# A modulation product moved from TensorE's narrow tiles to VectorE, one half of it

## The reference, cut to what matters

```python
mod = jnp.einsum('bd,de->be', jax.nn.silu(c), w_ada[l]) + b_ada[l]
sh1, sc1, g1, sh2, sc2, g2 = [m[:, None, :] for m in jnp.split(mod, 6, axis=-1)]
h = _rms(x, norm1_g[l]) * (1.0 + sc1) + sh1
```

## Time and profile before

| what | value |
|---|---|
| median of 3 runs | 1909.57 us (1907.05 to 1909.94) |
| profiled execution, its span | 1910.2 us |
| TensorE busy | 1819.2 us (95%) |
| VectorE busy | 601.7 us (31%) |
| ScalarE busy | 477.1 us (25%) |
| read from main memory | 579.96 MB |

### The profile page before, as it was taken

One profiled execution on the slowest core, in us unless ns is written; L12 is line 12 of the kernel. 1 busy time (PEld: TensorE's weight loads), 2 busy tenths in 40 slices (PEclk: granted clock), 3 DMA queues, 4 the chain that ended last, 5 costly groups with the idle time before them and its releaser, 6 DMA issues.

```text
span 1910.2 us, 27104 instructions
## 1 busy us (share of the span) xinstructions
PE 1819.2 (95%) x11233; PEld 1032.4 (54%) x11233; DVE 601.7 (31%) x1224; ACT 477.1 (25%) x800; POOL 351.5 (18%) x306
## 2 busy tenths in 40 slices
PE   8999999999998899999999999999999898899998
PEld 8987999777976333323332233322322697644443
DVE  6777555337566300100010000000000787501112
ACT  5854443325322110000000010000000565322121
POOL 3000000000000599999940000000000100100000
PEclk9998999998999999999999999999999899999999
DMA  6555657446733999999999999999999451579996
GB/s 196 156 142 185 198 197 239 153 134 212 263 111 132 394 419 415 420 419 420 412 418 420 420 418 408 419 420 420 415 418 402 111 168 62 220 308 420 420 419 281
DMA packets 152740, 582.89 MB, mean 305 GB/s; under 512 B 11673, under 2 KB 77866, under 8 KB 109600
## 3 DMA queue, kind: packets, MB, share of 16 engines
q1 hardware_dynamic: 150000, 575.09, 77.3%
q0 software_dynamic: 2608, 5.97, 1.2%
HBM read 579.96 MB, written 1.05 MB: 304 GB/s over the span
## 4 chain that ended last, share of the span: by engine, by line
PE 75%; DMA 14%; DVE 7%; ACT 3%; issue 2%; SPq 0%; ACTq 0%; DVEq 0%
PE ps L1814 18%; PE ps L437 9%; PE ps L438 9%; PE ps L439 9%; DMA ring<-in_moe_w_out 8%; PE ps L2312 6%; PE ps L1807 5%; PE ps L1846 4%; PE ps L2336 3%; DMA ring<-in_moe_w_in 3%; PE ps L2275 2%; PE ps L1726 1%; DVE wlo L480 1%; PE ps L1850 1%; DMA more<-in_moe_w_in 1%
## 5 line engine op out<-in xcount | busy, mean ns | idle before, releaser
L1814 PE MATMUL ps<-ring,xg 128*64 128x512 f32 x1638 | 405.8, 597 | 5.4 <-DMA ring<-in_moe_w_in 2.7
L480 DVE TENSOR_TENSOR wlo<-raw,whi 128x2048 fp32r<-128x2048 f32 (+5 forms) x95 | 209.5, 2208 | 175.9 <-ACT whi L462 175.6
L1814 PEld LDWEIGHTS ps<-ring,xg 128*64 128x64 f32 x1638 | 121.2, 136 | 248.0 <-issue 240.6
L462 ACT ACTIVATE whi<-raw 128x2048 fp32r<-128x2048 f32 (+4 forms) x96 | 177.0, 1847 | 176.9 <-PE ps L439 82.2
L437 PE MATMUL ps<-xh,whi 128*128 128x272 f32 (+1 forms) x712 | 210.4, 296 | 0.9 <-DVE wlo L857 0.9
L1846 PE MATMUL ps<-ring,ahm 128*64 128x512 f32 x808 | 203.5, 597 | 6.9 <-DMA ring<-in_moe_w_out 6.8
L439 PE MATMUL ps<-xh,wlo 128*128 128x272 f32 (+1 forms) x712 | 208.6, 293 | 0.0
L438 PE MATMUL ps<-xl,whi 128*128 128x272 f32 (+1 forms) x712 | 208.3, 293 | 0.0
L2237 POOL TENSOR_SCALAR lnt<-lnt,h 128x384 f32<-128x384 f32 x120 | 188.6, 1572 | 12.2
L1987 DVE TENSOR_TENSOR sgm<-sgm,ps 128x512 f32<-128x512 f32 x28 | 17.5, 683 | 496.7 <-PE ps L1814 496.7
L437 PEld LDWEIGHTS ps<-xh,whi 128*128 128x128 f32 (+1 forms) x712 | 133.4, 187 | 4.1 <-issue 2.4
(11 more groups left out here) (584 smaller groups left out, 2368.3 us busy)
## 6 DMA issues: line engine op xcount, KB each, us to landing
ring<-in_moe_w_in SPq DMA_DIRECT2D x117, 1024.0 KB, 19.9
ring<-in_moe_w_out SPq DMA_DIRECT2D x101, 1024.0 KB, 20.0
ring<-in_moe_w_in SPq DMA_DIRECT2D x117, 768.0 KB, 11.5
ring<-in_w_gate SPq DMA_DIRECT2D x29, 1024.0 KB, 13.1
raw<-in_ffn_w_in SPq DMA_DIRECT2D x28, 1024.0 KB
ring<-in_w_down SPq DMA_DIRECT2D x26, 1024.0 KB, 12.0
raw<-in_w_ada SPq DMA_DIRECT2D x24, 1024.0 KB
ring<-in_w_up SPq DMA_DIRECT2D x20, 1024.0 KB, 9.5
```

The lines of the kernel that those rows point to most:

```text
L462: e.activation(whi[0:rows, s % NSPL, 0:n], raw[0:rows, i % NRAW, 0:n], ACT.Copy).then_inc(S.hi.s, S.hi.up((s,)))
L480: e.tensor_tensor(wlo[0:rows, s % NSPL, 0:n], raw[0:rows, i % NRAW, 0:n], whi[0:rows, s % NSPL, 0:n].bitcast(F32), ALU.subtract).then_inc( ...
L1814: ins = e.matmul(ps_[b][64 * v:64 * v + 64, :], a[:, j, 64 * v:64 * v + 64], both[v][:, 0, 512 * b:512 * b + 512], start=j == 0, stop=j == 7)
```

## The change

Chunks 0 to 11 of the modulation product (half of it) leave the narrow tiles. Such a chunk now covers all 1024 rows and 256 columns, as eight blocks of 128 x 256, and VectorE sums the eight blocks, each times silu(c) of its rows as a scalar of the partition, into a 128 x 256 accumulator: one `tensor_scalar` and seven `scalar_tensor_tensor`, each waiting for the one before (`dve_ada_sum`). Two accumulators alternate; they are the two rows that `act_ada` used. TensorE adds up the partitions with two matmuls of one moving column of ones (`pe_ada_sum`); four chunks share a bank, ScalarE copies eight columns from it (`act_ada_sum`), and VectorE adds the bias once for all three groups.

In the list of chunks one ada chunk stands behind the up chunk of each of steps 1 to 12. `dve_ada_sum` for chunk j stands at the end of step j (0 to 11), in step 0 behind the end of the layer norm; `pe_ada_sum` for chunk j - 1 stands between the gate tiles and the up tiles of step j (1 to 12); `act_ada_sum` in ScalarE's steps 4, 8 and 12. The chunk's slot is now free when VectorE's sum is done. The narrow chunks after `gz` are now 12 and 13, the first of group 3; those after the keys and the column turn of group 2 are gone; 14 to 23 stay where they were. A chunk of the new form is read from memory in runs of 256 floats instead of 1024. The bytes are the same.

```diff
--- before.py
+++ after.py
@@ -23,7 +23,6 @@
 NRING1, NMORE1, CAP_A, CAP_B = 11, 1, 96, 64
 NP1 = 4
 GROUPS = [(0, 2048), (2048, 1536)]
-FFN_ADA = (4, 6, 8, 10)
 LAMBDA_INIT = 0.8 - 0.6 * math.exp(-0.3 * 0)
 STEPS = [(-90, 14), (-63, 13), (-45, 12), (-31, 11), (-22, 10), (-15, 9), (-11, 8), (-7, 7), (-6, 6), (-5, 5),
          (-4, 4), (-3, 3), (-2, 2), (-1, 1), (0, 0), (1, 17), (2, 18), (3, 19), (4, 20), (5, 21), (6, 22), (7, 23),
@@ -201,6 +200,9 @@

         for _ in range(n):
             j = next(n_ada)
+            if j < 12:
+                M.add(("ada", j), 128, CW, by_rows(w_ada, 256 * j, 8, 256), split=False)
+                continue
             part = w_ada[256 * (j % 4):256 * (j % 4) + 256, 1024 * (j // 4):1024 * (j // 4) + 1024]
             M.add(("ada", j), 128, CW, by_rows(part, 0, 2, 1024), split=False)

@@ -218,20 +220,18 @@
         M.add(("gt", j), 112, 2 * 3 * 336, gate_pieces(j), zero=True)
     for j in range(6):
         M.add(("gb", j), 128, 8 * 224, by_rows(w_rg, 224 * j, 8, 224))
-    plan_ada(2)
     for j in range(6):
         M.add(("ro", j), 112, CW, by_blocks(w_ro, j, 112), keep=True)
     for j in range(14):
         M.add(("ffn", "g", j), 128, CW, by_rows(d["ffn_w_in"][0], 256 * j, 8, 256))
         M.add(("ffn", "u", j), 128, CW, by_rows(d["ffn_w_in"][0], 3584 + 256 * j, 8, 256))
-        plan_ada(2 if j == 0 else 1 if j in FFN_ADA else 0)
-    plan_ada(2)
+        plan_ada(1 if 1 <= j <= 12 else 0)
     for j in range(14):
         M.add(("ffn", "d", j), 128, CW, by_blocks(d["ffn_w_out"][0], j, 128), keep=True)
     M.add(("gz", 0), 128, 128, by_rows(w_gl, 3072, 8, 16))
     for j in range(2):
         M.add(("gk", j), 128, CW, by_rows(w_gl, 512 + 256 * j, 8, 256))
-        plan_ada(2)
+        plan_ada(2 if j == 0 else 0)
     for j in range(2):
         M.add(("gq", j), 128, CW, by_rows(w_gl, 256 * j, 8, 256))
     plan_ada(2)
@@ -489,7 +489,9 @@
                 e.wait_ge(pe.s, pe.at("ring", R1.name, last_in(ring[:, 2 * NSPL + k, :])))
             if i >= NRAW:
                 p = S.chunks[i - NRAW][4]
-                if p is None or i - NRAW in S.kept:
+                if S.chunks[i - NRAW][0] in DVE_ADA:
+                    e.wait_ge(dve.s, dve.at(*S.chunks[i - NRAW][0]))
+                elif p is None or i - NRAW in S.kept:
                     e.wait_ge(S.pe.s, S.pe.at("used", i - NRAW))
                 else:
                     e.wait_ge(S.lo.s, S.lo.at(p))
@@ -590,14 +592,45 @@
     ada_row = [row1[:, 0:256], row1[:, 256:512]]
     quarters = idn.rearrange("p (c r) -> p c r", r=32)[:, :, 0]

+    DVE_ADA = [("ada", j) for j in range(12)]
+    ada_acc = ada_row
+
+    def dve_ada_sum(e, j):
+
+
+        i = M.index["ada", j]
+        w, o = raw[:, i % NRAW, :].rearrange("p (k n) -> p k n", k=8), ada_acc[j % 2]
+        if j == 0:
+            e.wait_ge(act.s, act.at("silc"))
+        if j >= 2:
+            e.wait_ge(pe.s, pe.at("adas", j - 2))
+        e.wait_ge(M.raw[i % NRAW].s, M.raw[i % NRAW].at(i))
+        e.tensor_scalar(o, w[:, 0, :], silp[:, 0, 0:1], None, ALU.mult).then_inc(dve.s, dve.up())
+        for k in range(1, 8):
+            e.wait_ge(dve.s, dve.n)
+            e.scalar_tensor_tensor(o, w[:, k, :], silp[:, k, 0:1], o, ALU.mult, ALU.add).then_inc(dve.s, dve.up(("ada", j)))
+
+    def pe_ada_sum(e, j):
+        g, r = j // 4, j % 4
+        p = bank("adas", g) if r else bank.take(e, "adas", g)
+        e.wait_ge(dve.s, dve.at("ada", j))
+        for i in range(2):
+            ins = e.matmul(p[:, 2 * r + i:2 * r + i + 1], ada_acc[j % 2][:, 128 * i:128 * i + 128], cst[:, C_SM + 1:C_SM + 2],
+                           start=True, stop=True)
+        ins.then_inc(pe.s, pe.up(("adas", j)))
+        if r == 3:
+            bank.give(("adas", g), (act, "adas", g))
+
+    def act_ada_sum(e, g):
+        e.wait_ge(pe.s, pe.at("adas", 4 * g + 3))
+        e.activation(modc[:, 8 * g:8 * g + 8], bank("adas", g)[:, 0:8], ACT.Copy).then_inc(act.s, act.up(("adas", g)))
+
     def pe_ada(e, j):


         g, r = j // 4, j % 4
         w = weights(e, M, ("ada", j)).rearrange("p (k n) -> p k n", k=2)
         p = bank("ada", g) if r else bank.take(e, "ada", g)
-        if j == 0:
-            e.wait_ge(act.s, act.at("silc"))
         for k in range(2):
             for c in range(4):
                 ins = e.matmul(p[32 * c:32 * c + 32, 0:256], silp[:, 2 * r + k, :], w[:, k, 256 * c:256 * c + 256],
@@ -608,7 +641,7 @@

     def act_ada(e, g):
         e.wait_ge(pe.s, pe.at("ada", g))
-        if g >= 2:
+        if g >= 5:
             e.wait_ge(pe.s, pe.at("adac", g - 2))
         e.activation(ada_row[g % 2], bank("ada", g)[:, 0:256], ACT.Copy).then_inc(act.s, act.up(("ada_row", g)))

@@ -905,8 +938,6 @@
                     ins.then_inc(pe.s, pe.up(("gt", 3 * j + mt, g), used(M, ("gt", j))))
                     bank.give(("gt", 3 * j + mt, g), (act, "gate", 3 * j + mt, g))
         pe_rg_in(e, "gb", "gelu")
-        for j in range(2):
-            pe_ada(e, j)
         acc = {(t, q): bank.take(e, "ln0", t, q) for t, _, _ in XTILES for q in range(2)}
         front = bank.take(e, "ln0", 2)
         for j in range(4):
@@ -1144,15 +1175,8 @@
                                   k == 0, k == 7)
                     ins.then_inc(pe.s, pe.up(("f" + nm, 2 * j + i), used(M, ("ffn", nm, j))) if i else pe.up(("f" + nm, 2 * j)))
                     bank.give(("f" + nm, 2 * j + i), (act, "fg", 2 * j + i) if nm == "g" else (dve, "fu", 2 * j + i))
-            if j == 0:
-                for i in (2, 3):
-                    pe_ada(e, i)
-            elif j in FFN_ADA:
-                pe_ada(e, 4 + FFN_ADA.index(j))
-            if j in (2, 12):
-                pe_ada_columns(e, j // 12)
-        for j in (8, 9):
-            pe_ada(e, j)
+                if nm == "g" and 1 <= j <= 12:
+                    pe_ada_sum(e, j - 1)
         acc = {(t, q): bank.take(e, "ln1", t, q) for t, _, _ in XTILES for q in range(2)}
         front = bank.take(e, "ln1", 2)
         for j in range(12):
@@ -1186,10 +1210,10 @@
                 if f >= 4:
                     e.wait_ge(dve.s, dve.at("fa", f - 4))
                 e.activation(g, bank("fg", f)[:, 0:T], ACT.Silu).then_inc(act.s, act.up(("fg", f)))
+                if f in (8, 16, 24):
+                    act_ada_sum(e, f // 8 - 1)
                 e.wait_ge(dve.s, dve.at("fu", f))
                 e.activation(fah[:, f, :], g, ACT.Copy).then_inc(act.s, act.up(("fa", f)))
-            if j in (0, 10):
-                act_ada(e, j // 10)
         for j in range(13):
             split_hi(e, M, s)
             s += 1
@@ -1217,8 +1241,11 @@
             if j == 0:
                 dve_ln_finish(e, "ln0", 0, TILES)
                 dve.label(("ln0", "full"))
-            if j in (3, 13):
-                dve_ada(e, j // 13)
+            if j < 12:
+                dve_ada_sum(e, j)
+            if j == 13:
+                e.wait_ge(act.s, act.at("adas", 2))
+                e.tensor_tensor(modc[:, 0:24], modc[:, 0:24], colA[:, 64:88], ALU.add).then_inc(dve.s, dve.up())
         for j in range(13):
             split_lo(e, M, s)
             s += 1
@@ -1287,7 +1314,7 @@
             ins = mm3(e, p, wh[:, k, :], wl[:, k, :], xh[:, k, :], xl[:, k, :], k == 0, k == 7)
         ins.then_inc(pe.s, pe.up(("gz",), used(M, ("gz", 0))))
         bank.give(("gz",), (act, "zT"))
-        for j in (10, 11):
+        for j in (12, 13):
             pe_ada(e, j)
         p = bank.take(e, "bg")
         e.wait_ge(landed["bgr"].s, landed["bgr"].at("all"))
@@ -1301,9 +1328,6 @@
             bank.give(("lg", hh), (dve, "lg", hh))
         pe_chan(e, "gk", 0)
         pe_chan(e, "gk", 1)
-        for j in (12, 13):
-            pe_ada(e, j)
-        pe_ada_columns(e, 2)
         pe_chan(e, "gq", 0)
         pe_chan(e, "gq", 1)
         for j in (14, 15):
@@ -1385,7 +1409,6 @@
     def act_gla(e, s):
         e.wait_ge(pe.s, pe.at("gz"))
         e.activation(zT[:, :], bank("gz")[0:16, 0:T], ACT.Copy).then_inc(act.s, act.up(("zT",)))
-        act_ada(e, 2)
         split_hi(e, M, s)
         s += 1
         e.wait_ge(dve.s, dve.at("E1"))
@@ -1473,7 +1496,6 @@
                 e.tensor_tensor(E4[:, m, :], p, E4[:, m, :], ALU.mult).then_inc(dve.s, dve.up(("gk", m)))
         split_lo(e, M, s)
         s += 1
-        dve_ada(e, 2)
         e.wait_ge(act.s, act.at("E3"))
         e.tensor_copy(decs, E3[:, :, 16:272].rearrange("p h (c s) -> p h c s", s=64)[:, :, :, 63]).then_inc(dve.s, dve.up(("decs",)))
         e.wait_ge(dve.s, dve.at("decs"))
```

## The result

The changed kernel takes 1918.35 us (median of 6 runs, 1914.92 to 1928.58) against 1909.76 for the kernel before beside it (6 runs, 1907.05 to 1914.4): ratio 1.0042, 95% interval 1.0021 to 1.0062. So the change costs 7 to 8 us, slower by more than the 0.2% that can be told from no change. By the ratio, the 1909.57 of before become 1917.6, near the upper end of the forecast: 1913.7 in a range of 1909 to 1918, with slower the likeliest of the three. The cost is nearly twice the 4.1 us that were forecast.

A forecast was written before the change was run, and what follows sets the result against it. TensorE was taken to bound the kernel (busy 95% of 1910.2 us). Terms: -12.0 + 5.3 + 6.5 + 1.3 + 3.0 = +4.1 us, so 1909.57 becomes 1913.7, range 1909.0 to 1918.0.

The forecast's parts named there:

- What goes and what comes: On TensorE: narrow chunks and turns leave, 12.0 us ahead of the keys, 2.5 behind; twelve sums of 0.44 add 5.3.
- The chain: On VectorE: eight dependent operations per sum take 4.1 us (3.4 to 4.8), nearly hidden in steps 1 to 11.
- The room in a step: Steps 1 to 11: the chain ends 0.3 us before TensorE asks for it, so no wait.
- The first wait: Step 1: TensorE waits 6.5 us (5.8 to 7.2) for chunk 0's sum, which stands behind the layer norm on VectorE.
- The stage behind: From bg to gv 0: no wait at bg, 1.5 us gained before gq 0 despite a new 1.5 wait; +1.3 in all.
- The bank count: Linear attention: group 3's bank, taken behind gz, is come upon by the second tile of gv 0, not the third.
- the clock: Behind the two long waits: TensorE at half clock for 3 us of work, costing 1.6 and 1.4 us, 3.0 together.
- The sum, with these put right: Whole kernel: the forecast's terms summed to +4.1 us, from 1909.57 to 1913.7.
- second wait: Second tile of gv 0: TensorE waits about 4.0 us instead of 1.2 for ScalarE's copy of group 3's row; +2.8.
- The second: Rival: both waits are there, but the clock stays up or its low stretches fall into them; 1910.7 us, chance 0.22.
- The third: Rival: VectorE's chain also holds TensorE in steps 1 to 11, at 0.60 us an operation; 1918.1 us, chance 0.13.
- The fourth: Rival: the waits are not there; 1905.6 us without the first, 1901.4 without the second as well; chance 0.10.

The follow-up runs named there:

- e5: Changed kernel with the layer norm's end in step 13 and narrow chunks 12 and 13 behind the keys, nothing behind gz; 1900.91 us (0.9947), again 1903.24 (0.9958).
- e1: Changed kernel with the end of the layer norm moved from step 0 to step 13; 1912.0 us, ratio 1.0009 to the kernel before.
- e3: Changed kernel with the layer norm's end in step 13 and ScalarE's copy of group 3's row ahead of the split of gv 2; 1903.08 us, ratio 0.9962.
- b2: Kernel before, with the end of the layer norm in step 13 behind the bias of the modulation group; 1911.34 us, ratio 1.0003.
- e6: Changed kernel with four more operations (times 1.0) on VectorE at the end of each sum; 1932.21 us, one run.
- e4: Changed kernel with eight f32 matmuls that compute nothing ahead of TensorE's wait for the first sum; 1917.14 us, ratio 1.0037.
- e2: Changed kernel with ScalarE's copy of group 3's row ahead of the split of gv 2 instead of behind it; 1913.83 us, ratio 1.0013.
- b1: The first control: kernel before, with the end of the layer norm moved to step 13, ahead of the modulation group's bias; 1921.68 us, ratio 1.0052.
- e7: Changed kernel with the sum of chunk 0 ahead of the end of the layer norm in step 0; 1920.17 us, one run.

## Why the prediction was right, and where its sizes were off

**What goes and what comes, right.** The sum's two matmuls cost 0.44 in each of the eleven undisturbed steps, as taken: a step takes 12.55 us, and 96 x 0.126 + 0.44 is 12.54, so nothing else slows it. That the narrow chunks were worth 12.0 and 2.5 is borne out by their balance in e5: 8.2 by the terms, 8 to 10 measured. Its single terms were not timed apart, but at the down product the traces without the first wait (e1, e3 and both of e5) start at 339.8 to 341.8 and the kernel before and b2 at 348.6 and 346.7: 7.0 apart in the mean, for 12.0 - 5.3 = 6.7.

**The chain, right.** 3.99 us for 4.1. The room in a step, forecast as 0.3, is 0.26 by e6, and no sum but the first waited. The Trainium skill (VectorE: DVE Perf Modes, section on the TRN2 errata) has a cycle table that would have made the chain 2.6, an estimate; below the table the same section says that this row is too short for a single operation and gives, as measured, (N + 151) / 0.96 ns for an f32 `tensor_tensor`, by which it would be 3.4, also an estimate. The trace agrees with neither: (3.61 - 0.50) / 6 = 0.52 from start to start where they have 0.33 and 0.42. The nearest row of the trace was the better guide.

**The first wait, right.** 6.49 for 6.5, at the place and by the releaser named, and e1 shows that it is the norm ahead of the sum.

**The stage behind, mechanism right, one size a little low.** The wait at `bg` is gone. VectorE's chain from `bg` to the low half of gq 0 is as long as before (457.86 to 472.76 here, 459.31 to 474.22 before: 14.9), and the start of gq 0 came 1.0 nearer to `bg`, 1.5 with the wait ahead of `bg`, as forecast. The wait there was 1.27 for 1.5 in this trace; in e1, e3 and e4 it was 2.8, where no low stretch of the clock lay ahead of it, and gq 0 started 17.25 us behind `bg` in all of them. The 1.5 thus rest on a low stretch that the traces of before and after happen to share. The bank count was right: the second tile of gv 0, and e2 removes it. Its wait was 4.57 and 4.1 for 4.0: the bank came back 9.35 and 8.86 us behind the start of the pair, for 8.8.

**The term that was mis-sized: the clock.** It had 1.6 and 1.4, from a 3 us stretch at half speed. The stretch behind either wait is 5 us long here, and e1 and e4 put the first at 2.4. The second stage lost 24.03 - 18.24 = 5.8 against 2.8 + 1.4 = 4.2; with 3.4 of it idle (4.57 for 1.19), the clock is 2.4, and against e2 it is 24.03 - 16.79 - 4.57 = 2.7. So the two make about 4.8 and not 3.0. The size isn't a constant either: behind the 6.9 us of b1 the low stretch was 3 us long, as in the earlier trace rows.

**A term that was missing: two waits for a bank.** The prediction says that behind the feed-forward block only two waits of TensorE bear on the edit, and finds none ahead of it. Two more did, 0.84 and 0.85 us before the last of the eight turned tiles (L730), at 166.15 and 451.65; they are in all three traces of the kernel before and its controls and in none of the ten of the changed one. At both places the kernel before holds a bank for a group of narrow chunks, so that the eighth tile comes upon the bank of the first; that this is the reason follows from the order of `take` and was not tested. TensorE gets from the seventh tile to the next product 0.35 and 0.47 sooner (2.30 to 1.95 and 2.31 to 1.84), 0.8 in all.

**The sum, with these put right.** 4.1 + 1.8 for the clock + 0.6 for the longer second wait - 0.8 = +5.7. The routing starts 5.0 and 7.7 us late, and the times say +8.0 (4.0 to 11.8) and +7.1 (3.8 to 10.5). The mechanism was right. That the range held, with 0.4 to spare by the ratio (the median itself is 1918.35), is in part luck: two terms were off, and two executions of one kernel differ by more than that.

**Low stretches that have no wait.** Both changed traces lose another 1.6 to 3.1 us between the column turn and the routing, where TensorE has no new wait: 118.14 and 119.67 us against 116.56. A window of the changed kernel:

```profile
550.60:571.20 20.60, 20.60 (x110) 13.46 (x110) 15.75 (x42) 2.48 (x3) 0.00 (x0) 0.92 0.29 101
```

and the same work in the kernel before:

```profile
547.20:567.00 19.80, 19.80 (x118) 12.85 (x116) 16.38 (x44) 2.57 (x3) 0.00 (x0) 1.00 0.30 104
```

The change doesn't bring this one. From the column turn to the first product that waits for vt takes 64.5 us with the stretch and 62.9 without. It is there in both changed traces, in e1 to e4 and e6, and also in b2 (64.48), a kernel without the change; it is missing in the kernel before, b1 and both of e5, and in e7 (62.85), which has the change and a long second wait. So it comes with and without the change, 1.6 us each time. The same holds before 172 us: the ten traces with the change have the same program there, and their first product of step 0 starts between 162.53 and 165.28. Why the clock falls there stays open.

**The rivals.** The second, a clock that stays up, is refuted by the windows. The third, a chain that holds every step, needed e6's longer chain to come true. The fourth turned on whether the sum stood behind the norm. It did here, and made otherwise, in e3, the time is 7 us under the kernel before; the forecast for it had been 1901.4, 8.2 under. The reads in runs of 256 floats and the sums aren't what makes the change slower: both are in e5, too, and the steps of 12.55 us leave no room for a cost of the reads there.

## What to carry to other kernels

Moving work from the bound engine to an idle one pays only if its result is consumed late enough. Look at what stands ahead of it in the idle engine's queue in the **first** step, where prologue work still lies, not only in the steady ones. A short instruction that gives a PSUM bank back belongs ahead of any long one that may wait for a load or that nobody needs soon; here and in the first control a copy of 0.38 and an addition of 0.15 us held TensorE for 4.6 and 6.9. And price a wait of TensorE of several us at its length plus 1.5 to 2.7 us of clock behind it, not at its length; part of that can come back where low stretches then fall otherwise.

## What the runs showed of the hardware

- Behind idle stretches of 6.5 and 4.6 us on TensorE the granted clock was 0.50 for the next 5 us of full work, then 1.00 again. The same time filled with matmuls that compute nothing left the clock at 1.00 and was worth 2.4 us in the stage. The length varies: behind 6.9 us (b1) and 7.3 us of idleness it was 3 us of work at 0.50, and behind 2.1 us (e7) it was 3 us too. The Trainium skill (TensorE: Matmul & The Clock Gate, section on HAM oscillation) says that an idle TensorE starts its next work cold; the trace agrees.
- The clock also falls to half in places where TensorE has no wait at all, for instance 0.92 in the mean over 20 us of full work at 550.6. One kernel differs from one execution to the next in this, and b2, without the change, has the same stretch. Where such a stretch lies ahead of a wait for another engine it costs nothing: the wait for gq 0 was 1.3 with it and 2.8 without, and gq 0 started at the same distance from `bg`. In the traces without it there, it came behind gq 0 and cost 1.5 (14.16 us from gq 0 to gv 0 against 15.67).
- A sum that has to wait is also slower itself. In e6 it starts 1.09 us behind the last gate matmul where it was 0.13, and takes 0.61 and not 0.50: of the 1.06 that each step is longer, 0.95 are the later start and 0.11 the slower sum.
